# A transformer pair in fp32 on one core: re-timed order of work in the gated delta stage, with its beta and decay product turned over

## What is computed

```python
proj = x @ w_in                      # q, k, v (4096 columns), z (2048), b (16), a (16)
qkv  = silu(causal_depthwise_conv(qkv, conv_w))        # width 4
q, k = l2norm of each head, 8 heads of 128;  v: 16 heads of 128
beta = sigmoid(b);  g = -exp(a_log) * softplus(a + dt_bias);  g = cumsum(g) in a chunk of 64
decay = exp(g[c] - g[s]) for c >= s
A     = strict_lower(beta * (k k^T) * decay);  t_inv = (I + A)^-1
u, w  = t_inv @ (beta v), t_inv @ (beta k exp(g))
per chunk: v_new = u - w S;  o = (q exp(g)) S + (q k^T * decay) v_new
           S = S exp(g_last) + k_tail^T v_new
o = rmsnorm(o) * norm_w * silu(z);   result = o @ w_out   # 2048 -> 1024
```

## Time and profile before

| | us |
|---|---|
| median of the runs shown | 1746.82 |
| the profiled execution's own time | 1748.16 |
| its span in the trace | 1746.5 |
| mean granted TensorE clock | 0.969 |
| PE busy | 1665.5 (95%) |
| DVE, ACT, POOL busy | 1012.4, 882.2, 162.9 |
| the gated delta stage in the trace | about 689 to 1045 |

### The profile page before, as it was taken

The page is one execution under the profiler, slowest core; times in us unless marked ns, Lnnn a source line. Parts: engine busy times, 40 slices in busy tenths (PEclk is TensorE's granted clock), DMA queues, the critical chain, the costliest instruction groups (busy, mean ns, idle before and its releaser), DMA issues.

```text
span 1746.5 us, 25817 instructions
## 1 busy us (share of the span) xinstructions
PE 1665.5 (95%) x10243; PEld 1369.9 (78%) x10243; DVE 1012.4 (58%) x1565; ACT 882.2 (51%) x1372; POOL 162.9 (9%) x176
## 2 busy tenths in 40 slices
PE   6999999999999999997888899999999899899998
PEld 4888888888888888776677788888877687678887
DVE  4555576655465555677344466554656545656663
ACT  5544455545364545654334345443667432456662
POOL 1000001000000000121232110000210000002220
PEclk9999999999999999999988899999999899999999
DMA  7666565655666565443111258655532212355552
GB/s 231 184 185 189 169 217 170 201 184 184 190 196 188 182 193 171 139 141 97 57 33 35 61 167 220 187 187 181 162 108 85 62 49 86 121 155 176 184 176 94
DMA packets 208635, 261.78 MB, mean 150 GB/s; under 512 B 21708, under 2 KB 145027, under 8 KB 208515
## 3 DMA queue, kind: packets, MB, share of 16 engines
q1 hardware_dynamic: 208514, 260.12, 48.3%
HBM read 259.01 MB, written 1.05 MB: 149 GB/s over the span
## 4 chain that ended last, share of the span: by engine, by line
PE 85%; DVE 8%; ACT 2%; POOL 2%; issue 2%; DVEq 0%; ACTq 0%; POOLq 0%
PE acc L452 24%; PE acc L454 23%; PE acc L453 23%; DVE low L427 2%; DVE gdn_cv L1317 2%; PE tr L698 1%; PE aux L2525 1%; ACT high L417 1%; PE aux L985 1%; PE tr L526 1%; PE tr L3275 1%; PE tr L1692 1%; PE aux L1000 0%; PE tr L1705 0%; PE aux L993 0%
## 5 line engine op out<-in xcount | busy, mean ns | idle before, releaser
L427 DVE TENSOR_TENSOR low<-raw,high 128x1024 fp32r<-128x1024 f32 (+1 forms) x487 | 589.8, 1229 | 427.1 <-ACT high L417 426.2
L417 ACT ACTIVATE high<-raw 128x1024 fp32r<-128x1024 f32 (+1 forms) x487 | 502.5, 1047 | 368.6 <-PE acc L454 353.6
L452 PE MATMUL acc<-high,xh 128*128 128x512 f32 (+1 forms) x1360 | 548.4, 403 | 7.4 <-DVE low L427 6.2
L454 PE MATMUL acc<-high,xl 128*128 128x512 f32 (+1 forms) x1360 | 532.1, 391 | 0.0
L453 PE MATMUL acc<-low,xh 128*128 128x512 f32 (+1 forms) x1360 | 530.9, 390 | 0.0
L452 PEld LDWEIGHTS acc<-high,xh 128*128 128x128 f32 x1360 | 260.4, 191 | 63.7 <-issue 7.1
L454 PEld LDWEIGHTS acc<-high,xl 128*128 128x128 f32 x1360 | 259.6, 191 | 54.2
L453 PEld LDWEIGHTS acc<-low,xh 128*128 128x128 f32 x1360 | 260.7, 192 | 48.7 <-issue 0.7
L452 PE MATMUL acc<-high,hh 128*128 128x512 f32 x472 | 185.7, 393 | 0.0
L454 PE MATMUL acc<-high,hl 128*128 128x512 f32 x472 | 183.9, 390 | 0.0
L453 PE MATMUL acc<-low,hh 128*128 128x512 f32 x472 | 183.7, 389 | 0.0
(11 more groups left out here) (449 smaller groups left out, 1727.7 us busy)
## 6 DMA issues: line engine op xcount, KB each, us to landing
raw<-in_ffn_w_gate_up SPq DMA_DIRECT2D x352, 256.0 KB, 3.2
raw<-in_ffn_w_down SPq DMA_DIRECT2D x176, 256.0 KB, 3.1
raw<-in_gdn_w_in SPq DMA_DIRECT2D x96, 256.0 KB, 3.0
raw<-in_ffn_up SPq DMA_DIRECT2D x88, 256.0 KB, 3.2
raw<-in_w_in SPq DMA_DIRECT2D x72, 256.0 KB, 2.9
raw<-in_sc_w_in SPq DMA_DIRECT2D x48, 256.0 KB, 3.1
raw<-in_ffn_down SPq DMA_DIRECT2D x44, 256.0 KB, 2.9
raw<-in_gdn_w_out SPq DMA_DIRECT2D x32, 256.0 KB, 3.0
```

Source lines behind the costliest of these rows:

```text
L417: nc.scalar.activation(high[t % HIGHS][:, 0:n], raw[t % RAWS][:, 0:n], ACT.Copy).then_inc(high_ready, 1)
L427: nc.vector.tensor_tensor(low[t % RAWS][:, 0:n], raw[t % RAWS][:, 0:n], high[t % HIGHS][:, 0:n].bitcast(F32), ALU.subtract).then_inc(low_r ...
L452: nc.tensor.matmul(o, a, wh, start=(k0 + kk == 0), stop=False)
L454: mm = nc.tensor.matmul(o, b, wh, start=False, stop=(k0 + kk == k - 1))
```

## The change

The gated delta stage is reordered. (a) The products of `gdn_ba` take the weights as stationary side (128 by 32) and the activations as moving side (128 columns), so that the result has its 32 channels on the partitions. ScalarE copies it, TensorE turns it back, and the gates start from there; the two sums of g move behind the first value of group 1 and their `exp` to group 2; beta's inverse moves from GpSimd to VectorE. (b) decay and decay_turned of the first four heads are done beside groups 6 and 7, in four halves on one bank, `aux[1]`. (c) GpSimd spreads `gm` after group 5. (d) `turn(R - 2)` stands in round R, ahead of the decays, in place of `turn(R - 1)` at the end of the round, and VectorE does normed, grams and scores in separate steps. (e) The diagonal blocks of `U` go from GpSimd to ScalarE. (f) The fill is dealt anew: 6 units ahead of the rounds (7 before), then 8, 9, 9 and 8 in the rounds (7, 6, 6, 6) and 8 beside the last (16). The output product's first four tiles no longer wait for the last inverse, and its two groups use banks [0, 1] and [2, 3]. (g) `place` gives a group the pair that the group ahead of it does not use, which swaps the pairs for every group from `mix_pr0` to the kernel's end. What is computed stays the same.

The diff without the new semaphores and the parts that only repeat a step for another engine:

```diff
             elif first.get("mix_low", len(groups)) <= gi <= first.get("mix_pn1", -1):
                 place.append([0, 1])
+            elif g[0] == "gdn_out":
+
+                place.append([2 * (gi - first["gdn_out"]) + t for t in range(TB)])
             else:
-                place.append([2 * (gi % 2) + t for t in range(TB)])
+                low_pair = gi == 0 or 2 in place[-1] or 3 in place[-1]
+                place.append([0, 1] if low_pair else [2, 3])
...
-            FILL = ((0, 0, 0, 1, 1, 1, 1, 1, 1, 1, 0, 0, 0),) + 3 * ((1, 1, 1, 1, 0, 0, 1, 1, 0, 0, 0, 0, 0),)
-            LAST = (2, 2, 2, 2, 0, 2, 2, 2, 2)
+            FILL = ((1, 1, 1, 1, 1, 1, 1, 0, 0, 0, 0, 1, 0),) + 2 * ((1, 1, 1, 1, 0, 1, 1, 1, 0, 0, 1, 1, 0),) + (
+                (1, 1, 1, 1, 0, 0, 0, 0, 1, 1, 1, 1, 0),)
+            LAST = (1, 1, 1, 1, 1, 1, 1, 1, 0)
...
+            def channel_rows_pe(self, pe):
+                gi = self.ba
+                (t,) = tiles_of[gi]
+                n = 2 * VH
+                pe.wait_ge(low_ready, t + 1)
+                for tb in range(TB):
+                    if earlier[gi][tb]:
+                        pe.wait_ge(left(gi, tb), earlier[gi][tb])
+                    o = at_acc(gi, tb)[0:n, 0:P]
+                    for k in range(DC):
+                        wh = high[t % HIGHS][:, k * n:(k + 1) * n]
+                        wl = low[t % RAWS][:, k * n:(k + 1) * n]
+                        a, b = (x[:, k, tb * P:(tb + 1) * P] for x in (xh, xl))
+                        nc.tensor.matmul(o, wh, a, start=(k == 0), stop=False)
+                        nc.tensor.matmul(o, wl, a, start=False, stop=False)
+                        mm = nc.tensor.matmul(o, wh, b, start=False, stop=(k == DC - 1))
+                    mm.then_inc(acc_ready[tb], 1)
+
+            def turn_gates_pe(self, pe):
+                gi = self.ba
+                n = 2 * VH
+                for tb in range(TB):
+                    wait_left(pe, gi, tb)
+                for tb in range(TB):
+                    mm = nc.tensor.transpose(aux[1][:, 64 + tb * n:64 + (tb + 1) * n], self.sq[0:n, tb * P:(tb + 1) * P],
+                                             ident[0:n, 0:n])
...
             def gates_act(self, act):
                 gi = self.ba
-                act.wait_ge(self.g_nrs, 1)
                 for tb in range(TB):
                     act.wait_ge(acc_ready[tb], gi + 1)
-                    nc.scalar.activation(self.s_e[:, tb, 0:VH], at_acc(gi, tb)[:, 0:VH], ACT.Exp,
+                    nc.scalar.activation(self.sq[0:2 * VH, tb * P:(tb + 1) * P], at_acc(gi, tb)[0:2 * VH, 0:P],
+                                         ACT.Copy).then_inc(left(gi, tb), 1)
+                act.wait_ge(self.g_nrs, 1)
+                act.wait_ge(self.g_ba_psum, 1)
+                for tb in range(TB):
+                    nc.scalar.activation(self.s_e[:, tb, 0:VH], aux[1][:, 64 + 2 * VH * tb:64 + 2 * VH * tb + VH], ACT.Exp,
                                          scale=self.nrs[:, tb:tb + 1]).then_inc(self.g_e1, 1)
...
+            def decay_sums_act(self, act):
                 act.wait_ge(self.g_G_psum, 1)
                 nc.scalar.activation(self.s_eg[:, :], aux[1][:, 0:VH], ACT.Exp).then_inc(self.g_eg_ready, 1)
                 nc.scalar.activation(self.s_etail[:, :], aux[1][:, VH:2 * VH], ACT.Exp).then_inc(self.g_eg_ready, 1)
...
                 nc.vector.tensor_scalar(self.s_beta[:, :, :], self.s_e[:, :, 0:VH], 1.0, None, ALU.add).then_inc(self.g_beta1, 1)
+                dve.wait_ge(self.g_beta1, 1)
+                nc.vector.reciprocal(self.s_beta[:, :, :], self.s_beta[:, :, :]).then_inc(self.g_beta_ready, 1)
...
-            def gates_pool(self, pool):
-                pool.wait_ge(self.g_beta1, 1)
-                nc.gpsimd.tensor_tensor(self.s_beta[:, :, :], self.s_beta[:, :, :],
-                                        minus1[:, 0:TB * VH].rearrange("p (t h) -> p t h", t=TB), ALU.pow).then_inc(self.g_beta_ready, 1)
...
+                self.channel_rows_pe(pe)
+                for g in range(1, 8):
                     if g == 1:
+                        products(pe, self.qkv[g], xh, xl, at_=1, then=lambda: self.turn_gates_pe(pe), at2=2,
+                                 then2=lambda: self.pairs_pe(pe, 0))
                         pe.wait_ge(self.g_g_ready, 1)
                         nc.tensor.matmul(aux[1][:, 0:VH], upto[:, :], self.s_g[:, 1, :], start=True, stop=True)
                         nc.tensor.matmul(aux[1][:, VH:2 * VH], beyond[:, :], self.s_g[:, 0, :], start=True, stop=True).then_inc(self.g_G_psum, 1)
-                    self.pairs_pe(pe, 2 * g - 2)
-                for g in range(1, 8):
-
-                    products(pe, self.qkv[g], xh, xl, at_=2, then=lambda: inside(g))
+                    else:
+                        products(pe, self.qkv[g], xh, xl, at_=2, then=lambda: self.pairs_pe(pe, 2 * g - 2), at2=2,
+                                 then2=lambda: self.first_decay_pe(pe, 2 * (g - 6)) if g >= 6 else None)
                     self.pairs_pe(pe, 2 * g - 1)
+                    if g >= 6:
+                        self.first_decay_pe(pe, 2 * (g - 6) + 1)
                 fill = self.fill_pe(pe)
-                for s, n in ((14, 1), (15, 2), (16, 2)):
+                for s, n in ((14, 1), (15, 2), (16, 1)):
                     self.some(fill, n)
                     self.pairs_pe(pe, s)
-                self.decay_pe(pe, 0)
-                self.some(fill, 1)
-                self.decay_turned_pe(pe, 0)
                 self.grams_pe(pe, 0)
-                self.some(fill, 1)
+                self.some(fill, 2)
...
+                    if g == 2:
+                        self.decay_sums_act(act)
                     high_to(act, tiles_of[gi][1] + AHEAD)
                     if g:
                         self.pairs_act(act, 2 * g - 2)
+                    if g >= 6:
+                        self.first_decay_act(act, 2 * (g - 6))
...
                         self.pairs_pool(pool, 2 * g - 1)
-                self.spread_pool(pool, 0)
-                self.inv.pool(pool, 0)
+                    if g == 5:
+                        self.spread_pool(pool, 0)
+                        self.inv.pool(pool, 0)
                 self.mask_pool(pool, 0)
...
-                    if R < self.NB:
-                        self.last_pool(pool, R)
...
-                pe.wait_ge(self.g_U_corner, 2 * self.NB)
                 body, _ = tail_of(self.out)
                 for t in body[:8]:
+                    if t == body[4]:
+                        pe.wait_ge(self.g_U_corner, 2 * self.NB)
...
+                    self.last_diag_act(act, B)
...
+                else:
+                    for _ in range(2):
+                        yield
+                for h in range(2):
+                    if R >= 2:
+                        self.turn_pe(pe, R - 2, h)
+                    yield
                 if R + 1 < self.NB:
                     self.decay_pe(pe, R + 1)
...
-                if 0 < R < self.NB:
-                    for h in range(2):
-                        self.turn_pe(pe, R - 1, h)
-                        yield
...
+                else:
+                    for _ in range(2):
+                        yield
+                for h in range(2):
+                    if R >= 2:
+                        self.turn_act(act, R - 2, h)
+                    if R and h == 0:
+                        self.square_act(act, R - 1)
+                    yield
                 if R + 1 < self.NB:
                     self.decay_act(act, R + 1)
-                if R:
-                    self.square_act(act, R - 1)
...
-                yield
+                else:
+                    for _ in range(2):
+                        yield
+                for h in range(2):
+                    if R >= 2:
+                        self.turn_dve(dve, R - 2, h)
+                    if R and h:
+                        self.mean_dve(dve, R - 1)
+                    yield
                 if R:
-                    self.mean_dve(dve, R - 1)
+                    self.normed_dve(dve, R - 1)
+                yield
                 yield
                 if R + 1 < self.NB:
                     self.grams_dve(dve, R + 1)
-                if R:
-                    self.normed_dve(dve, R - 1)
+                yield
+                yield
                 if R + 1 < self.NB:
                     self.scores_dve(dve, R + 1)
                 yield
-                if 0 < R < self.NB:
-                    for h in range(2):
-                        self.turn_dve(dve, R - 1, h)
-                        yield
...
+            def first_decay_pe(self, pe, i):
+                a = i % 2
+                pe.wait_ge(self.g_gm_ready, 8)
+                if i == 0:
+                    pe.wait_ge(self.g_t3out, 8)
+                elif i == 1:
+                    pe.wait_ge(self.g_D_ready, 1)
+                else:
```

(51 more changed lines are left out.)

45 lines of the change are left out of this document (21 added, 24 removed).

## The result

The changed kernel takes 1735.0 us (1730.3 to 1736.0) against 1747.8 (1745.0 to 1748.8): a ratio of 0.9924, 95% interval 0.9902 to 0.9946. That is 12.7 us less, where the forecast had 27.5. The profiled execution has 1734.76 us, its span 1733.0.

The account below looks back on a forecast made before the run. PE bounds the kernel, busy 95% of the span. Stage terms (198.65 - 169.8 - 0.4, less 3) give 25.4, with the Mixer 27.5, so 1746.82 falls to 1719.3 us; range 1709 to 1737.

Parts of the forecast that it names:

- the allowance of 3: Deduction of 3 us from the forecast gain for stretches at the lower clock level that could not be placed.
- the first rival: Lower level or VectorE takes part back: falls in R0, R1, R2 and LAST, 13 in all, 1732 us; chance 0.24.
- The turn as price: In the rounds PE waits for GpSimd's gate, 13.3 us in three waits; of one 4.76 only 0.8 the turn's alone.
- Round 3: Inverse round priced at 32.5 us: middle round 25.9 less 5.4 for decays, plus 1.0 for turns and 11.0 for fill.
- no more than 2.2 us stand ahead of an X or U: In the rounds, most VectorE work ahead of an X or U once normed, grams and scores take separate steps.
- out1 to turn(3, 0): Behind the last round: the chain square, mean, root, normed, gate takes 12.5 us, with 1.8 of new PE wait.
- Round 0: First inverse round priced at 33.2 us: 19.4, 8 units at 11.0, and 2.8 for steps 7 to 10 without a unit.
- Nothing, or 0.3 us a round either way: In the rounds, the cost or gain of moving the diagonals from GpSimd's pair to two ScalarE instructions.
- The value groups: Moved first decays add 6.4 us over two groups; step 0 starts at 827.1, some 0.4 late, bounds -5 and +6.
- the rival built on it: ScalarE's tables in the value groups: a switch costs 1.4 more than the load, 5.5 us, 1725 us; chance 0.03.
- Beta and decay: Products of gdn_ba in the new form: no change taken, zero gain, bounds 2.5 us less to 5.8 more.
- The Mixer: PE's 2.48 us wait for a bank VectorE still reads shrinks with the other pair: 2.1 us less.

Follow-up runs that it names:

- old_rounds: Changed kernel with the order of the rounds (turns, mean, grams, normed, scores, fill shares) put back as before: 1739.4 us, ratio 0.9953 to the kernel before.
- dve_order: Changed kernel with VectorE's grams, normed and scores all back in step 10 of rounds 0 to 2, turns still moved: 1736.6 us, ratio 0.9944.
- r3_norm: Changed kernel with VectorE's normed of round 2 moved from step 8 to step 10 of round 3: 1726.4 us, ratio 0.9883.
- last_chain: Changed kernel with round 3's squares and mean put ahead of turn(2, 0)'s copy and low part behind the last round: 1724.4 us, ratio 0.9885.
- fill0: Changed kernel with round 0's eight units of fill beside steps 0 to 4, 6, 8 and 10: 1728.0 us, ratio 0.9891.
- diag_pool: Changed kernel with U's diagonal blocks written by GpSimd again, behind the gate: 1739.1 us, ratio 0.9946.
- all3: Changed kernel with three edits at once, to round 3's normed, the last round's squares and mean, and round 0's fill: 1717.7 us, ratio 0.9822.

## Why the prediction was right or wrong

In the profiled executions the change is 13.4 us where 27.5 were forecast: 14.1 missing. 10.8 are the rounds (13.8, less the allowance of 3), 1.2 step 0, 2.1 the tail. The time, 1735.0, is at the upper end of the range (1709 to 1737), where the first rival stood (1732) and not the forecast; and two of the signs of being wrong were there, waits of over 1 us for X and windows at 0.5 in the rounds.

- **The turn as price:** right. The three waits are gone, old_rounds brings them back, 11.1 us. That only 0.8 of the 4.76 us are the turn's alone is not borne out: with the turn moved and VectorE's old order, dve_order, PE waits 1.0 and 2.2 us in rounds 1 and 2, and the rounds lose 3.7 of the 11.1. VectorE's order without the moved turn was not run.
- **Round 3: the step that failed.** "25.9 - 5.4 + 1.0 + 11.0" took the decays out of the sum as work and forgot that they were cover. Without them VectorE's root wait, normed and `low` lie bare ahead of X(5). The prediction's sentence "no more than 2.2 us stand ahead of an X or U" was counted for rounds with a decay and left out waits; it was 4.8. Round 2 has the same root wait (1.39 us before 932.23) and normed ahead of its X, but no `low` there, and 2.05 us of products of decay_turned stand beside them (from 932.33), so that PE waits for neither. That these products were the cover is read from the trace; no run put products into round 3's gap. Missed: 8.7, of which r3_norm gives back 6.4; the 2.3 that are left stay open.
- **out1 to turn(3, 0):** the wait was named, at 1.8; it is 3.6. The chain was taken as 12.5, shorter than today's 13.25; it is 14.3, since turn(2, 0) and turn(2, 1) had moved into it on ScalarE and VectorE. I had priced these moves on PE only. The stretch at 1.2 GHz behind it wasn't in the sum. last_chain gives back 3.8, and its tail is 2.8 shorter.
- **Round 0:** 33.2 against 34.9; on VectorE the grams in step 10 (2.16 us at 849.28) and a `low` behind them (1.22 at 851.36) had no unit beside them, against the 0.7 us a step that the forecast took. It had 2.2 us ahead of an X or U in its own text. fill0: 2.9.
- **Round 1** and **values0 to out1** were right within 0.1. **Round 2** is 1.7 long; 1.2 of it is part (e), which delays a `high`. "Nothing, or 0.3 us a round either way" was wrong twice: it costs this wait, and diag_pool shows that without it GpSimd would cost up to 2.6.
- **The lower level:** allowed 3 us; in the rounds of the changed kernel, the stretch at 1010 with them, PE spends 23.9 us at 1.2 GHz, 12 lost. That is what the first rival says ("13 in all: 1732"), in other places. In round 3 it is the wait and not a lack of wide products: r3_norm leaves the products as they are, and the stretch goes. In round 0 the two aren't told apart; all3 has as many steps without a unit there, though not in a row, and keeps 1.00.
- **The value groups:** step 0 at 828.2 (827.1 forecast). The `exp` and its load are as priced:

```profile
806.52 1.28 ACT L1746 ACT_TABLE_LOAD   x1
807.81 0.60 ACT L1746 ACTIVATE gdn_qk<-aux 128x512 f32<-128x512 f32 x1
```

The `exp` starts 0.01 us behind the load. The Trainium skill ("ScalarE: Activation LUTs", What ACT_TABLE_LOAD costs) adds a drain of 1380 ns to each switch; these rows show none, and the rival built on it is out. That 828.2 is so near to 827.1 is partly luck: the stage's first wait of over 1 us ends 3.7 us sooner than before (part (a), counted as zero), and what follows takes 4.8 more than the forecast (113.3 us against 108.5), with the 17.1 us at 1.2 GHz in it that the forecast lacked.
- **Beta and decay:** "zero" can't be told from the 1.0 us in the time and is wrong in the marks (some 4 by 715, 1.7 by step 0). The price I took was the old one; the products are at the cheap end of my bounds.
- **The Mixer:** the wait fell from 2.48 to 0.3 and is worth its 2.1 (in all3 PE is at its place 482.0 us behind turn(3, 0), before 484.1). In the changed kernel the tail is no shorter, since the 1.2 GHz stretch behind the gate's wait and a longer one at 1270 (10.2 us, before 6.8) take it back.

The pieces of the forecast sum to 169.8 us, and all3 takes 169.9. That is partly luck, as rounds 2 and 3 are still 1.7 and 2.3 over and round 0 and the last piece 1.5 and 2.0 under; but the gain was in the new order, and short pieces of work on VectorE and ScalarE in three places stood in its way.

## What to carry to other kernels

When a step is taken out of a round, list what it covered on the other engines, and walk the queue of each engine once for the round that lacks it (the first, the last) rather than for the middle one alone. Price a moved step on every engine that works on it. And expect the clock to give or take some us elsewhere: compare the marks around the edited piece, and the time at the lower level apart, before a median that moves less or more than they do is explained.
